# Recurrent heads in pairs: denominators from columns of ones, gate rows spread by DMA, and the value units moved between the convolved tiles

## The chip, the cores and the metric

One Trainium2 chip, one core of it. The metric is the device time of one execution in microseconds (us); lower is better. TensorE does the matmuls, VectorE, ScalarE and GpSimd the elementwise work, and DMA queues issued from SyncE and ScalarE move data between HBM and the on-chip memory SBUF. Matmul results land in one of eight PSUM banks.

## The reference, cut to what matters

A model of three blocks over 512 tokens of width 1024 runs in one kernel: a recurrent layer, a band attention layer, and a layer with differential and forgetting attention, each with a gated feed-forward part. The change lies in the first layer. There the input is normalised and projected to q, k, v, an output gate o, eight gate values per token and the queries of a small memory attention. q and k pass a causal convolution of four taps and a SiLU. Four heads of width 192 then run a stabilised mLSTM. In parallel form, with F the running sum of the log forget gates, a = i - F the gate column and M the running maximum of a:

```python
S[s, t] = (k_s . q_t) * 192**-0.5 * exp(-(M_t - a_s))     # for s <= t, else 0
num_t = sum_s S[s, t] * v_s
den_t = sum_s S[s, t]
h_t = num_t / max(|den_t|, exp(-(F_t + M_t)))             # then an RMS norm per head
out = h * rsqrt(mean(h*h) + 1e-6) * head_g * sigmoid(o)
```

The kernel normalises num itself with den inside the epsilon term, so that one root per head and token serves both. The memory attention is an ordinary softmax over 256 memory tokens for two pairs of heads. Its result and the four heads' outputs are concatenated and multiplied by w_out.

## The kernel before, in words

Tokens lie on the free axis (512) and features on the 128 partitions; only the value tiles have tokens on partitions. Large products run on f32 operands split into a high part (WH, hH) and a low part (WL, hL), three matmuls for each 128 rows. The weights come in units of 256 columns, loaded by SyncE into `raw`; ScalarE copies a unit into WH and VectorE writes WL, the difference (step `conv`, L1221 and L1578), two slots in turn. A feature-major tile (`fm`, L891) is 24 matmuls of 512 columns, a value tile (`tm`, L910) 48 matmuls of 256 columns.

A function `order()` writes one list of steps, and each engine walks through it and issues its own part of every step. So every engine's queue has the order of that list, and an engine that waits at a step holds all that it has behind it. Bank numbers are handed out in turn over eight banks, and TensorE waits until the engine that drained the bank's last content is through.

The steps around the change are these.
- `conv_in` for each tile of q and k: VectorE multiplies the PSUM tile by the norm factor (L1553), ScalarE starts the convolution (L1300), VectorE adds three taps (L1701). The SiLU (L1307) is put off to the end of the next tile.
- `probs`, `norm_p`, `turn`, `values`, `parts`: the memory attention. VectorE takes maxima (L1712) and negates them (L1731), ScalarE the exponentials (L1335), VectorE normalises (L1739, L1755), TensorE transposes (L1024), ScalarE and VectorE copy the two banks of it to SBUF (L1359, L1765), and TensorE multiplies by the values (L1044). `soft()` puts them between tiles of other work, as many tiles as its argument `per` says for each of four rounds.
- `gates_*`: four rows of gate values are worked out on four partitions; the E row is exp(-(F + M)).
- `m_scores` for a head: TensorE spreads the M row over 128 partitions by a matmul with one row of the identity (L1054) and computes the scores, pieces of 128 and 64 rows in turn (L1065); ScalarE copies the M row out, VectorE subtracts, ScalarE takes the exponential, VectorE multiplies it with the scores, GpSimd zeroes the upper triangle.
- `m_values`: TensorE multiplies by the values (L1086), by a matrix of ones for the denominators (L1093), and spreads the E row (L1100). `m_sums`: sums of squares over the head by a matmul with ones (L1110), then denominators, root and reciprocal (L1828). `gated`: the product with sigmoid(o), GpSimd (L2077), and its split.
- `out_first`: the first product with w_out (L835) over five of eight feature tiles, kept in four banks; `out_rest` adds the other three.

The work is done in this order: two tiles of q, two of k, two and two more, value units 0 and 1, q, k, then the heads one by one between value unit 2 and the six tiles of o.

Of the kernel before, what the change touches and what calls it, by code (L numbers as in the profile page):

```python
# [7 lines left out]
F32 = mybir.dt.float32  # L8
# [18 lines left out]
POS = {j: bi * 512 + off for j, L, bi, off in JL}  # L27
HALVES = ((0, 6, (4, 4, 4)), (6, 11, (4, 3, 3)))
# [14 lines left out]
def plan():  # L43
# [3 lines left out]
    u += [("a_w_in", 0, 0, 8, 256 * j, 256) for j in (0, 3, 1, 4, 6, 7, 2, 5, 8, 9, 10, 11)]  # L47
# [97 lines left out]
def order():  # L145
# [5 lines left out]
    def put(*x):  # L151
        steps.append(x)
# [209 lines left out]
    put("fence", "memA")  # L362

# [4 lines left out]
    gens = qk(0) + qk(1) + [g_tm(2, "mix0", "vA", "v")] + qk(2) + [g_tm(1, "mix0", "vA", "v", u0=2)]  # L368
# [8 lines left out]
    for hd in range(4):  # L377
        fill(gens, tiles[hd][0])
        if hd < 3:
            put("m_scores", hd + 1)  # L380
        fill(gens, tiles[hd][1])
        put("m_values", hd)
        deferred.append(("m_sums", hd))
        fill(gens, tiles[hd][2])
        if hd == 2:
            for t in range(3):
                put("gated", t)
# [151 lines left out]
def program(nc, wall, xt, memt, colsd, biasd, consts, rope, out):  # L539
    ctx = ExitStack()  # L540
    with ctx:
# [41 lines left out]
        vA = place("vA", [128, 4, 768])  # L583
# [3 lines left out]
        Mrow = place("Mrow", [4, 512])  # L587
        colA = place("colA", [128, 4, 4])
        Erow = place("Erow", [4, 512])
# [14 lines left out]
        top[0] = mark_M  # L604
        den = [place(f"den{i}", [128, 512]) for i in range(2)]
        fac = [place(f"fac{i}", [128, 512]) for i in range(2)]
        Mb = [place(f"Mb{i}", [128, 512]) for i in range(2)]
        Eb = place("Eb", [128, 1280])
        Pm = [place(f"Pm{i}", [128, 1280]) for i in range(2)]
# [55 lines left out]

        rows = nc.dram_tensor("rows", (8, 512), F32, kind="Internal").ap()
# [5 lines left out]
        gz, gt, ga, gm = O[0:4, 1, :], O[0:4, 2, :], O[0:4, 3, :], Mrow[:, :]  # L672
# [12 lines left out]
        s_rows = sem("rows")  # L685
        s_cols, s_K, s_RC, s_RS, s_out = (sem(n) for n in ("cols", "consts", "RC", "RS", "out"))
# [99 lines left out]
        def tensor(e):  # L786
# [52 lines left out]
            for what, *a in STEPS:  # L839
# [208 lines left out]
                elif what == "m_scores":  # L1048
                    hd = a[0]
                    b, before = bank(("mb", hd), ("Mb", hd))  # L1050
                    if before:
                        w.wait_ge(*at(*before))
                    w.wait_ge(*at("gateD", "mm"))
                    e.matmul(ps[b][:, :], ident[0:4, hd:hd + 1].broadcast_to([4, 128]), gm, start=True,  # L1054
                             stop=True).then_inc(*mark("mspread", hd))
                    ends = {bi: [x[0] for x in JL if x[2] == bi][-1] for bi in range(3)}
                    bs = [bank(("ms", hd, bi), ("mP", hd, ends[bi])) for bi in range(3)]
                    for j, L, bi, off in JL:
                        b, before = bs[bi]
                        if before:  # L1060
                            w.wait_ge(*at(*before))
                        for n, (t, r, _, _) in enumerate(pieces(hd)):
# [3 lines left out]
                                          q[r, t, j * 128:512], start=(n == 0), stop=(n == 1))  # L1066
                        mm.then_inc(*mark("mscores", hd, j))

                elif what == "m_values":
                    hd = a[0]  # L1070
                    P = Pm[hd % 2]
                    w.wait_ge(*at("mtri", hd, JL[-1][0]))
                    for t0 in (0, 2):
                        for un in range(192 * hd // 256, (192 * hd + 191) // 256 + 1):
                            w.wait_ge(*at("vev", "vA", t0, un))
                    for t, r, c0, width in pieces(hd):
                        if r.start == 64:
                            b = BANK[("mv", t)]
                            turns.append(b)
                        else:  # L1080
                            held = width == 64
                            b, before = bank(("mv", t), ("mnum", t, 64 if held else 0), hold=held)
                            if before:
                                w.wait_ge(*at(*before))
# [3 lines left out]
                        mm.then_inc(*mark("mvalues", t, r.start))  # L1088
# [1229 lines left out]
```

## Time and profile before

| | us |
|---|---|
| median of 3 runs | 1922.43 (1920.96 to 1923.5) |
| the profiled execution | 1919.19 |
| its span, first to last instruction | 1917.4 |
| TensorE busy | 1875.5 |
| VectorE busy | 927.4 |
| ScalarE busy | 753.3 |
| GpSimd busy | 277.8 |

The profile calls TensorE PE, its weight loads PEld, VectorE DVE, ScalarE ACT, GpSimd POOL and SyncE SP; L891 is line 891 of the kernel. A matmul in plain f32 leaves two records. A releaser behind an arrow is the instruction whose end let the idle engine go on.

### The profile page before, as it was taken

How to read it: one execution, taken by the hardware profiler on the slowest of the kernel's cores; microseconds unless marked ns; L12 is line 12 of the kernel's file. 1: busy time of each engine (PE TensorE's matmuls, PEld its weight loads, DVE VectorE, ACT ScalarE, POOL GpSimd, SP SyncE). 2: the span in 40 equal slices, each digit the busy share in tenths (PEclk: the TensorE clock that was granted, in tenths of full speed). 3: DMA queues.
4: the chain of work that ended last, by engine and by line, in shares of the span. 5: the costliest groups of instructions: out<-in, count | busy, mean ns of one | idle time of the engine just before them, and what ended most of it. 6: DMA issues, size and time to landing. Idle time of an engine off the chain costs nothing.

```text
span 1917.4 us, 21811 instructions
## 1 busy us (share of the span) xinstructions
PE 1875.5 (98%) x8962; PEld 1513.6 (79%) x8962; DVE 927.4 (48%) x1443; ACT 753.3 (39%) x1190; POOL 277.8 (14%) x239
## 2 busy tenths in 40 slices
PE   9989999999999999999999999999999999999998
PEld 7775568888888889667888888877887788888886
DVE  6754565544345343664545245355566443323324
ACT  5553444432133234574433133342457442312323
POOL 1001121221022110001222012122000122201210
PEclk9999999999999999999999999999999999999999
DMA  5121012222222333211232222222122123232221
GB/s 219 66 88 45 22 66 93 86 107 104 94 88 87 111 111 124 96 45 66 88 110 92 106 88 92 94 100 89 66 78 77 66 89 110 88 107 91 88 94 61
DMA packets 30754, 172.30 MB, mean 90 GB/s; under 512 B 3256, under 2 KB 5432, under 8 KB 12736
## 3 DMA queue, kind: packets, MB, share of 16 engines
q1 hardware_dynamic: 26320, 163.03, 23.9%
q10 hardware_dynamic: 4336, 7.88, 1.2%
q8 instruction: 71, 1.16, 0.2%
q14 instruction: 27, 0.22, 0.0%
HBM read 168.79 MB, written 2.11 MB: 89 GB/s over the span
## 4 chain that ended last, share of the span: by engine, by line
PE 88%; DVE 5%; ACT 4%; issue 1%; DMA 1%; POOL 0%; ACTq 0%; SPq 0%; DVEq 0%; POOLq 0%
PE ps L891 49%; PE ps L1148 18%; PE ps L835 6%; PE ps L910 5%; PE ps L1044 2%; PE ps L999 2%; DVE WL L1578 1%; PE ps L1065 1%; PE ps L1024 1%; PE ps L1086 1%; ACT PB L1335 1%; DMA raw<-in_wall 1%; ACT WH L1221 1%; PE ps L824 1%; PE ps L815 0%
## 5 line engine op out<-in xcount | busy, mean ns | idle before, releaser
L891 PE MATMUL ps<-hH,WH 128*128 128x512 f32 x1472 | 581.4, 395 | 7.0 <-DVE WL L1578 5.8
L891 PE MATMUL ps<-hH,WL 128*128 128x512 f32 x1472 | 573.7, 390 | 0.0
L891 PE MATMUL ps<-hL,WH 128*128 128x512 f32 x1472 | 573.5, 390 | 0.0
L1578 DVE TENSOR_TENSOR WL<-raw,WH 128x1024 fp32r<-128x1024 f32 (+2 forms) x312 | 382.2, 1264 | 375.7 <-ACT WH L1221 375.6
L1221 ACT ACTIVATE WH<-raw 128x1024 fp32r<-128x1024 f32 (+2 forms) x312 | 303.6, 1021 | 285.7 <-PE ps L1148 228.4
L891 PEld LDWEIGHTS ps<-hH,WH 128*128 128x128 f32 x1472 | 276.8, 188 | 76.4 <-issue 16.9
L891 PEld LDWEIGHTS ps<-hL,WH 128*128 128x128 f32 x1472 | 276.8, 188 | 58.8 <-issue 2.6
L891 PEld LDWEIGHTS ps<-hH,WL 128*128 128x128 f32 x1472 | 276.6, 188 | 58.1
L1148 PE MATMUL ps<-fH,WH 128*128 128x512 f32 x528 | 205.4, 389 | 0.0
L1148 PE MATMUL ps<-fL,WH 128*128 128x512 f32 x528 | 205.4, 389 | 0.0
L1148 PE MATMUL ps<-fH,WL 128*128 128x512 f32 x528 | 205.4, 389 | 0.0
L2093 POOL TENSOR_TENSOR Y<-Y,Rsb 128x512 f32<-128x512 f32 x66 | 85.2, 1292 | 548.3 <-ACT Y L1427 382.8
L1148 PEld LDWEIGHTS ps<-fH,WH 128*128 128x128 f32 x528 | 99.1, 188 | 20.6
L1148 PEld LDWEIGHTS ps<-fH,WL 128*128 128x128 f32 x528 | 99.1, 188 | 20.5
L1148 PEld LDWEIGHTS ps<-fL,WH 128*128 128x128 f32 x528 | 99.1, 188 | 20.5
L1437 ACT ACTIVATE fH<-Z 128x512 fp32r<-128x512 f32 x66 | 41.7, 632 | 186.1 <-DVE Z L1874 186.1
L2101 POOL TENSOR_TENSOR fL<-Z,fH 128x512 fp32r<-128x512 f32 x66 | 85.2, 1291 | 199.0 <-ACT fH L1437 199.0
L1553 DVE TENSOR_TENSOR GG<-ps,Rsb 128x512 f32<-128x512 f32 x66 | 45.5, 690 | 115.6 <-PE ps L891 107.3
L1874 DVE TENSOR_TENSOR Z<-ps,Y 128x512 f32<-128x512 f32 x66 | 45.3, 687 | 113.8 <-PE ps L891 108.2
L910 PE MATMUL ps<-WH,hH 128*128 128x256 f32 x320 | 92.8, 290 | 3.9 <-ACT PA L1335 3.9
L910 PE MATMUL ps<-WL,hH 128*128 128x256 f32 x320 | 91.2, 285 | 0.0
L910 PE MATMUL ps<-WH,hL 128*128 128x256 f32 x320 | 91.2, 285 | 0.0
(343 smaller groups left out, 2047.8 us busy)
## 6 DMA issues: line engine op xcount, KB each, us to landing
raw<-in_wall SPq DMA_DIRECT2D x140, 1024.0 KB, 4.6
raw<-in_wall SPq DMA_DIRECT2D x12, 768.0 KB, 3.9
bias<-in_bias ACTq DMA_DIRECT2D x12, 256.0 KB, 3.4
X<-in_xt SPq DMA_DIRECT2D x8, 256.0 KB, 9.6
CB<-rows ACTq DMA_DIRECT2D x8, 256.0 KB, 3.4
out_y<-X SPq DMA_DIRECT2D x3, 512.0 KB, 3.0
raw<-in_wall SPq DMA_DIRECT2D x4, 256.0 KB, 5.5
mrA<-in_memt ACTq DMA_DIRECT2D x4, 256.0 KB, 6.0
```

The source lines that it names most:

```text
L835: mm = e.matmul(ps[b][:, :], ww[:, k, c:c + 128], x, start=(k == seq[0] and i == 0), stop=(k == seq[-1] and i == 2))
L891: mm = e.matmul(ps[b][:, 0:N], ww[:, k, c:c + 128], x[:, k, 0:N], start=(k == 0 and i == 0), stop=(k == 7 and i == 2))
L910: mm = e.matmul(o, x[:, k, t * 128:t * 128 + 128], ww[:, k, :], start=(k == 0 and i == 0), stop=(k == 7 and i == 2))
L999: mm = e.matmul(ps[b][:, c:c + L], queries[u["kind"]][r, u["m"], t * 128:t * 128 + 128], keys[u["kind"]][r, u["m"], 0:L], start=opens, sto ...
L1148: mm = e.matmul(ps[b][:, :], ww[:, kx, mi * 128:mi * 128 + 128], x[:, k, :], start=(gi == 0 and kx == 0 and p == 0), stop=(gi == 2 and kx ...
L1221: e.activation(WH[n % NCV][:, c], raw[n % NRAW][:, c], ACT.Copy).then_inc(*mark("wh", n, x))
L1437: e.activation(F[i]["H"][:, k, :], F[i]["Z"][m % 2][:, :], ACT.Copy).then_inc(*mark("fH", i, int(half), k))
L1553: return e.tensor_tensor(dst, src, Rsb[rows, :], ALU.mult)
L1578: e.tensor_tensor(WL[n % NCV][:, c], raw[n % NRAW][:, c], WH[n % NCV][:, c].bitcast(F32), ALU.subtract).then_inc(*mark("wl", n, x))
L1874: e.tensor_tensor(F[i]["Z"][m % 2][:, :], ps[BANK[(name, m)]][:, :], F[i]["Y"][m % 4][:, :], ALU.mult).then_inc(*mark("fz", name, m))
L2093: e.tensor_tensor(y[:, :], y[:, :], Rsb[:, :], ALU.mult).then_inc(*mark("fy", i, m))
L2101: e.tensor_tensor(F[i]["L"][:, k, :], F[i]["Z"][m % 2][:, :], F[i]["H"][:, k, :].bitcast(F32), ALU.subtract).then_inc(*mark("fL", i, int(h ...
```

## The change

- The M and E rows are written to a small DRAM tensor and read back by DMA, spread over partitions, on ScalarE's queue (`m_rows`, `m_row`). The matmuls at L1054 and L1100 go.
- The value tile `vA` grows from 768 to 1024 columns. Beside each 64-wide piece of a head stand 64 columns of ones, so that the matmul of this piece gives the numerators on 64 partitions and the denominators on the other 64. The matmuls at L1093 go. The evacuation of the value tiles is cut where the ones stand (`V_PARTS`).
- Scores of two heads are computed together: first all 128-row pieces, then the 64-row pieces in turn between the two heads, which lie on different halves of the partitions.
- The sum of squares takes its second operand from `den`, half of which holds the squared denominator, scaled; the add on VectorE goes. `m_sums` is no longer put off, and `m_norm` is a step of its own.
- Three buffers for the products instead of two and a shared one; `m_prep` works out the exponentials ahead of the scores.
- The three value units stand between the q and k tiles; the rounds of the memory attention get other numbers of tiles, and the steps of the heads are written out. Two fences, at which engines waited for one another, go.

```diff
-    u += [("a_w_in", 0, 0, 8, 256 * j, 256) for j in (0, 3, 1, 4, 6, 7, 2, 5, 8, 9, 10, 11)]
+    u += [("a_w_in", 0, 0, 8, 256 * j, 256) for j in (0, 3, 6, 1, 4, 7, 2, 5, 8, 9, 10, 11)]
...
-        return [(t, slice(0, 128), 192 * hd, 128), (t + 1, slice(0, 64), 192 * hd + 128, 64)]
-    return [(t + 2, slice(0, 128), 192 * hd + 64, 128), (t + 1, slice(64, 128), 192 * hd, 64)]
+        return [(t, slice(0, 128), 256 * hd), (t + 1, slice(0, 64), 256 * hd + 128)]
+    return [(t + 2, slice(0, 128), 256 * hd + 128), (t + 1, slice(64, 128), 256 * hd)]
+V_PARTS = [(0, 0, 192, 0), (0, 192, 64, 320), (1, 0, 256, 384), (2, 0, 64, 640), (2, 64, 192, 832)]
+V_ONES = ((192, 128), (704, 128))
...
-            timed.extend([[1, ("gates_later",)], [2, ("gates_rest",)], [9, ("gate_columns",)]])
+            timed.extend([[1, ("gates_later",)], [2, ("gates_rest",)], [5, ("gate_columns",)], [6, ("m_rows",)]])
...
-    gens = qk(0) + qk(1) + [g_tm(2, "mix0", "vA", "v")] + qk(2) + [g_tm(1, "mix0", "vA", "v", u0=2)]
+    gens = qk(0) + vA(0) + qk(1) + vA(1) + qk(2) + vA(2) + [g_fm(3, "mix0", "o", "o")]
...
-    soft("A", gens, lambda p: (2, 2) if p < 3 else (2, 0), lambda p: conv_ahead(now["unit"] + 2) if p else None)
-    put("fence", "mlstm")
-    gens.append(g_fm(3, "mix0", "o", "o"))
-    tiles = ((0, 1, 0), (1, 1, 1), (0, 1, 1), (0, 0, 1))
+    def rows_out(p):
+        if p:
+            conv_ahead(now["unit"] + 2)
+        if p == 3:
+            for hd in (0, 1):
+                put("m_row", "M", hd)
+            put("m_row", "E", 0)
+    soft("A", gens, lambda p: ((1, 2), (2, 1), (1, 2), (1, 0))[p], rows_out)
+    put("m_prep", 0)
+    put("m_row", "E", 1)
+    put("m_row", "M", 2)
+    put("m_prep", 1)
+    put("m_row", "M", 3)
     put("m_scores", 0)
...
+    put("m_prep", 2)
+    fill(gens, 2)
+    put("m_values", 0)
+    put("m_values", 1)
+    put("m_prep", 3)
+    fill(gens, 2)
+    put("m_sums", 0)
+    put("m_sums", 1)
+    fill(gens, 1)
+    put("m_norm", 0)
+    put("m_norm", 1)
+    for hd in (2, 3):
+        put("m_row", "E", hd)
+    fill(gens, 1)
+    put("m_scores", 2)
+    fill(gens, 2)
+    put("m_values", 2)
+    put("m_values", 3)
+    fill(gens, 2)
+    put("m_sums", 2)
+    put("m_sums", 3)
+    for t in range(3):
+        put("gated", t)
+    fill(gens, 1)
+    put("m_norm", 2)
+    put("m_norm", 3)
     run_deferred()
     fill(gens, 99)
...
+                    for n in (0, 1):
+                        for hd, (j, L, bi, off) in ([(hd, v) for hd in (h0, h0 + 1) for v in JL] if n == 0 else
+                                                    [(hd, v) for v in JL for hd in (h0, h0 + 1)]):
...
+                            t, r, _ = pieces(hd)[n]
...
                             mm = e.matmul(ps[b][:, off:off + L], kk[r, t, j * 128:j * 128 + 128],
-                                          q[r, t, j * 128:512], start=(n == 0), stop=(n == 1))
+                                          q[r, t, j * 128:512], start=(n == 0 and off == 0),
+                                          stop=(n == 1 and j == M_ENDS[bi]))
...
-                            mm = e.matmul(ps[b][r, j * 128:512], vA[:, j, c0:c0 + width],
+                            mm = e.matmul(ps[b][:, j * 128:512], vA[:, j, c0:c0 + 128],
                                           P[:, POS[j]:POS[j] + 512 - j * 128], start=(j == 0), stop=(j == 3))
...
+                    w.wait_ge(*at("msqP", hd))
+                    e.matmul(ps[b][:, :], ones, msq[hd % 2][:, :], start=True, stop=False)
+                    w.wait_ge(*at("msqD", hd))
+                    w.wait_ge(*at("mden2", hd))
+                    e.matmul(ps[b][:, :], ones, den[hd % 2][:, :], start=False, stop=True).then_inc(*mark("msums", hd))
...
+                elif what == "m_rows":
+                    w.wait_ge(*at("gateD", "mm"))
+                    e.dma_start(m_rows[0:4, :], gm).then_inc(s_mrows, 16)
+                    w.wait_ge(*at("gateE"))
+                    e.dma_start(m_rows[4:8, :], gE).then_inc(s_mrows, 16)
...
+                            w.wait_ge(*at("mEbD", hd - 2, JL[-1][0]))
+                        e.dma_start(Mb[hd % 2][:, :], m_rows[hd:hd + 1, :].broadcast_to([128, 512])).then_inc(
+                            s_M[hd % 2], 16)
...
-                    e.activation(D, D, ACT.Square, scale=1e-3).then_inc(*mark("mden2", hd))
-                    w.wait_ge(*at("mfac", hd, 1))
-                    e.activation(Fc, Fc, ACT.Sqrt).then_inc(*mark("mfacA", hd))
+                    e.activation(den[hd % 2][r, :], den[hd % 2][r, :], ACT.Square, scale=3e-6 ** 0.5).then_inc(
+                        *mark("mden2", hd))
+                    w.wait_ge(*at("mfac", hd, 0))
+                    e.activation(fac[hd % 2][:, :], fac[hd % 2][:, :], ACT.Sqrt, scale=1.0 / 192).then_inc(
+                        *mark("mfacA", hd))
...
+                    e.tensor_scalar(fac[hd % 2][:, :], ps[BANK[("mq", hd)]][:, :], 192e-34, 192e35, ALU.max,
+                                    ALU.min).then_inc(*mark("mfac", hd, 0))
...
+                    for n, (c, size) in enumerate(V_ONES):
+                        e.memset(vA[:, :, c:c + size], 1.0).then_inc(*(mark("vones") if n else mark("vonesh")))
```

## Rows read from the trace of the kernel before

**Rows 1.** The page: busy us, share of the span, instructions; the last chain.
```profile
PE 1875.5 (98%) x8962; PEld 1513.6 (79%) x8962; DVE 927.4 (48%) x1443; ACT 753.3 (39%) x1190; POOL 277.8 (14%) x239
...
PE 88%; DVE 5%; ACT 4%; issue 1%; DMA 1%; POOL 0%; ACTq 0%; SPq 0%; DVEq 0%; POOLq 0%
```

**Rows 2.** TensorE's waits, 60 to 330 us: total us, times, longest.
```profile
PE ps L891 <- DVE WL L1578: 4.5, 2, 2.8
PE ps L910 <- ACT PA L1335: 3.9, 1, 3.9
PE ps L1044 <- DVE PTA L1765: 3.8, 1, 3.8
PE ps L1044 <- ACT PTA L1359: 1.7, 1, 1.7
PE ps L835 <- DVE WL L1578: 1.2, 1, 1.2
```

**Rows 3.** TensorE's timeline, 160 to 187 us: start, us, instruction.
```profile
160.35 1.12 PE L1054 MATMUL ps<-Mrow,K 4*128 4x512 f32 x2
161.40 5.95 PE L1065 MATMUL ps<-q,k 128*128 128x512 f32 x16
...
174.21 0.39 PE L910 MATMUL ps<-WH,hH 128*128 128x256 f32 x1
...
180.06 4.62 PE L1086 MATMUL ps<-Pm,vA 128*128 128x512 f32 x16
184.60 2.42 PE L1093 MATMUL ps<-Pm,K 128*128 128x512 f32 x8
186.96 1.12 PE L1100 MATMUL ps<-Erow,K 4*128 4x512 f32 x2
```

**Rows 4.** TensorE's timeline, one pair of band scores.
```profile
803.46 2.43 PE L999 MATMUL ps<-kB,qB 64*128 64x512 f32 x16
```

**Rows 5.** VectorE's timeline, 85 to 147 us.
```profile
85.95 0.68 DVE L1553 TENSOR_TENSOR sq<-ps,Rsb 128x512 f32<-128x512 f32 x1
...
93.57 0.17 DVE L1739 RECIPROCAL stA<-stA 128x4 f32<-128x4 f32 x1
...
96.09 2.35 DVE L1578 TENSOR_TENSOR WL<-raw,WH 128x1024 fp32r<-128x1024 f32 x2
98.36 1.28 DVE L1712 TENSOR_REDUCE stA<-ps 128x2 f32<-128x512 f32 x2
...
146.54 0.68 DVE L1765 COPY PTA<-ps 128x512 f32<-128x512 f32 x1
```

**Rows 6.** Stretches: busy us, then granted clock, DMA share, GB/s.
```profile
102.00:102.50 0.50, 0.50 (x4) 0.50 (x3) 0.00 (x0) 0.50 (x3) 0.00 (x0) 0.50 0.70 295
147.00:152.00 5.00, 4.63 (x20) 2.87 (x21) 3.18 (x4) 1.12 (x2) 0.00 (x0) 1.00 0.33 98
```

**Rows 7.** ScalarE's timeline, 99 to 116 us.
```profile
99.89 0.47 ACT L1335 ACTIVATE PA<-ps,stA 128x256 f32<-128x256 f32 x1 [5.39 <-DVE stA L1731]
...
103.40 0.24 ACT L1335 ACTIVATION_READ_ACCUMULATOR PA<-ps,stA 128x1 f32 x1
...
115.16 0.63 ACT L1294 ACTIVATE Erow<-O 4x512 f32<-4x512 f32 x1
115.70 0.80 ACT L1320 ACTIVATE vA<-ps,small 128x256 f32<-128x256 f32 x2
```

**Rows 8.** TensorE's timeline, values of memory pair 1 and tile k4.
```profile
147.37 1.94 PE L1044 MATMUL ps<-PTA,mvA 128*64 128x512 f32 x8 [3.80 <-DVE PTA L1765]
149.24 0.50 PE L891 MATMUL ps<-hH,WH 128*128 128x512 f32 x1
```

**Rows 9.** DMA issues: count, KB each, median us to landing.
```profile
CB<-rows ACTq DMA_DIRECT2D x8, 256.0 KB, 3.4
```

**Rows 10.** VectorE's timeline, normalising a head, and WL before the out tiles.
```profile
197.82 3.35 DVE L1828 RECIPROCAL fac<-fac 128x512 f32<-128x512 f32 x1 [0.69 <-ACT fac L1394]
...
277.44 3.78 DVE L1578 TENSOR_TENSOR WL<-raw,WH 128x1024 fp32r<-128x1024 f32 x2 [1.65 <-ACT WH L1221]
```

More of the change, by code:

```diff
@@ L685, in program @@
         s_rows = sem("rows")
+        s_mrows = sem("mrows")
+        s_M = [sem(f"M{i}") for i in range(2)]
+        s_E = [sem(f"E{i}") for i in range(2)]
         s_cols, s_K, s_RC, s_RS, s_out = (sem(n) for n in ("cols", "consts", "RC", "RS", "out"))
@@ L1048, in tensor @@
                 elif what == "m_scores":
[L1049 to L1062, printed above, removed]
+                    h0 = a[0]
+                    bs = {}
+                    for hd in (h0, h0 + 1):
+                        for bi in range(3):
+                            bs[hd, bi] = bank(("ms", hd, bi), ("mP", hd, M_ENDS[bi]))
+                    for n in (0, 1):
+                        for hd, (j, L, bi, off) in ([(hd, v) for hd in (h0, h0 + 1) for v in JL] if n == 0 else
+                                                    [(hd, v) for v in JL for hd in (h0, h0 + 1)]):
+                            b, before = bs[hd, bi]
+                            if before:
+                                w.wait_ge(*at(*before))
+                            t, r, _ = pieces(hd)[n]
                             w.wait_ge(*at("qk", "q", t))
@@ L1107, in tensor @@
                         w.wait_ge(*at(*before))
-                    for n, (t, r, _, width) in enumerate(pieces(hd)):
-                        w.wait_ge(*at("msqP" if width == 128 else "msqD", t, r.start))
-                        mm = e.matmul(ps[b][:, :], ones[r, :], sq[t % 2][r, :], start=(n == 0), stop=(n == 1))
-                        mm.then_inc(*mark("msums", hd, n))
+                    w.wait_ge(*at("msqP", hd))
[3 more added lines that the diff above has]
+                    e.matmul(ps[b][:, :], ones, den[hd % 2][:, :], start=False, stop=True).then_inc(*mark("msums", hd))
                 elif what in ("out_first", "out_rest", "out_all"):
@@ L1318, in scalar @@
                     p = ps[BANK[(name, t0, un)]]
+                    if name == "vA":
+                        for i in range(2):
+                            for n, (_, c, size, o) in enumerate([v for v in V_PARTS if v[0] == un]):
+                                last = i == 1 and c + size == 256
+                                e.activation(vA[:, t0 + i, o:o + size], p[:, 256 * i + c:256 * i + c + size],
+                                             ACT.Copy, scale=small[:, 4 + t0 + i:5 + t0 + i]).then_inc(
+                                    *(mark("vev", name, t0, un) if last else mark("vevh", name, t0, un, i, n)))
+                        continue
                     for i in range(2):
@@ L1827, in vector @@
                     w.wait_ge(*at("mfacA", hd))
-                    e.reciprocal(Fc, Fc).then_inc(*mark("mfac", hd, 2))
-                    w.wait_ge(*at("mfac", hd, 2))
-                    for t, r, _, width in pieces(hd):
-                        w.wait_ge(*at("msqP" if width == 128 else "msqD", t, r.start))
+                    e.reciprocal(Fc[:, :], Fc[:, :]).then_inc(*mark("mfac", hd, 1))
+                    w.wait_ge(*at("mfac", hd, 1))
+                    w.wait_ge(*at("msqP", hd))
@@ L1832, in vector @@
+                    for n, (t, r, _) in enumerate(pieces(hd)):
                         e.scalar_tensor_tensor(out=q[r, t, :], in0=q[r, t, :], scalar=col("hg", t, p=r),
                                                in1=Fc[r, :], op0=ALU.mult, op1=ALU.mult).then_inc(
[L1834 removed]
+                            *mark("mnorm", hd, n))
                 elif what == "gated":
@@ L2190, in program @@
                        for i, x in enumerate(CONV_SEQ)}
-        MSQ_SEQ = [(t, r.start, hd, n) for hd in range(4) for n, (t, r, _, _) in enumerate(pieces(hd))]
-        MSQ_BEFORE = {(t, r): [("cvD",) + CONV_SEQ[-1] + (3,), ("cvD",) + CONV_SEQ[-2] + (3,)] + [
-            ("msums", h2, n2) for t2, r2, h2, n2 in MSQ_SEQ if h2 < hd and t2 % 2 == t % 2]
-            for t, r, hd, n in MSQ_SEQ}
         ROPE_SEQ = [(n, m) for n in ("dq", "dk") for m in range(4)]
```

216 lines of the change are left out of this document (98 added, 118 removed).

## The prediction

> **What bounds the kernel now.** The page comes first: TensorE is busy 98% of the span and every other engine under half, and the chain that ended last is 88% TensorE [rows 1]. So a microsecond taken out of TensorE's stream counts, one taken from another engine counts only where TensorE waits for it. Next the list of TensorE's waits in the stretch that the change touches, 60 to 330 us [rows 2]: six waits, 15.1 us together. That is what reordering could win at most, besides matmuls that go.
>
> The profiled execution took 1919.2 us, its span being 1917.4; the median is 1922.4. The sum is made against the first and its difference is taken off the median.
>
> **What goes from TensorE's stream.** Matmuls overlap at their ends, so I price them from start to start. The stretch from 160 to 187 us shows each kind [rows 3].
> - The spread of the M row (L1054): 160.35 to 161.40, 1.05 us. Four heads, 4.20 us. A DMA takes its place.
> - The spread of the E row (L1100): the same operation and 1.12 us with its tail, as the other; 1.05 us, four times, 4.20 us.
> - The denominator matmuls with ones as weights (L1093): 184.60 to 186.96, 2.36 us, four times, 9.44 us. The values matmuls keep their number and columns. A piece 64 wide becomes one 128 wide, whose other half is ones; the 16 records of a head take 4.54 us now (180.06 to 184.60) though half of them are only 64 wide, so width costs nothing.
> - Scores: a head takes 5.88 us (5.95 less the 0.07 by which the next overlaps) for 2560 columns, of which the values matmuls make as many in 4.54. The old order alternates matmuls over 128 rows and over 64 rows. The new one runs both heads' 128-row pieces first: 2560 columns, which I price at 4.54. Then come the 64-row pieces, turn by turn on rows 0 to 63 and 64 to 127, each head in its own bank. The band scores in the second layer have exactly these lengths and this alternation: 2.43 us with the tail, 2.36 without, for 2560 columns, so two run side by side [rows 4]. A pair costs 6.90 instead of 11.76; two pairs save 9.72. Bounds: if the 64-row pieces don't overlap, 4.54 instead of 2.36, and the saving is 5.36; if nothing changes, 0.
> - Sums of squares: two matmuls of 512 columns before and after, one of them over 128 rows instead of 64; 0, by the values matmuls, which cost the same over half the width.
>
> Together 27.56 us.
>
> **The first waits stay.** Up to 69.16 us the queues are in the same order, so the 1.67 us wait for WL stays. Unit 6 is now value columns; unit 7's WL comes after both convolutions of k on VectorE as before and ends at 85.95 [rows 5]; TensorE can start at 85.05, with its first half, as before. It gets there after two value tiles (5.85 each, 174.21 to 180.06 [rows 3]), the scores of memory pair 1 (about 1.9) and the gate columns (0.4), at about 83.2. 1.8 instead of 2.82.
>
> **The value tile at 100.96** waited 3.87 us for exponentials, and after that idle time the granted clock was 0.50 up to 104.5, that is 1.2 instead of 2.4 GHz; matmuls came 0.21 us apart, against 0.12 later, some 16 of them, 1.5 us [rows 2, 6]. In the new order q2 stands there. The exponentials start right after VectorE's maxima and free the banks as TensorE needs them, about 0.4 us late.
>
> **The new stall: values of memory pair 0.** In step order the new kernel has q2, turn, q3, turn, values. The values wait for the last copy of turned probabilities on VectorE, which is queued behind two convolutions. The chain from VectorE's queue, all durations from [rows 5, 7]:
> - 85.95 WL of unit 7 done, where q2's product began before; 2.52 normalising pair 0 (93.57 to 96.09): 88.5; the maxima of pair 1, first half 1.28 and a negation 0.17: 90.0.
> - ScalarE: exponentials 3.6: 93.6; the value tile's evacuation, now four instructions, 1.2 (two take 0.80); E row's Exp 0.54; first half of WH of unit 8 1.0 (half of two halves at 2.0): 96.3. VectorE has idled since 91.4.
> - WL of unit 8 2.3 (96.09 to 98.36): 98.6; convolution q2 3.8 (85.95 to 93.57 are two): 102.4; copy 0.6; convolution q3 3.8; copy: values start 0.83 after that copy starts (146.54, 147.37), at 107.7 [rows 5, 8].
>
> TensorE is through with q3 and its turn at 98.5 (two tiles of 5.56, half of 149.24 to 160.35 [rows 3, 8], two turns of 0.8, the 0.4). Stall: 9.2 us, instead of 1.65. Before, two value tiles that cost VectorE nothing stood at this place. Bounds: 3.8 (only the last convolution is late, as at 147.37) and 12. I take 9.2, since each link has a row. Idle for so long, TensorE should come back at 1.2 GHz as at 100.96: 3.4 us at half rate, 1.7 us lost (0 to 3.4).
>
> The values of pair 1 waited 3.80 behind the convolution of q5 [rows 2]. Now the value tile precedes them; what is left is the copy, 0.8.
>
> **DMA rows.** Two stores and eight broadcasts issue on ScalarE's queue, whose eight CB issues have a median of 3.4 us to landing [rows 9]. M0 is issued near 130, VectorE needs it at 134; its exponential must anyway stand behind the value tile on ScalarE until 140, and the masked products are wanted only after q4 and q5, near 156. Hidden by those two tiles; without that cover 3.4 us a pair. The memsets of ones fit into GpSimd's free time before 14 us, ahead of its squares.
>
> **The sums.** They used to be put off by a tile. Now they follow k4, k5 at once, and the second matmul waits for ScalarE's square of the denominator. On ScalarE that stands behind the convolution of k5, whose first half waits for VectorE, busy with k4. From the rows: VectorE ends the masks of head 3 and WL 12 about 2.6 us before k5 is through, so k5's share begins 0.8 after it, ScalarE 0.7 later, then 0.8 and the square 0.6: the matmul 3 us after k5, of which 0.95 is the first matmul. Then head 1's square stands behind head 0's square root, which waits for a clamp on VectorE behind the rest of k5: another 1.7. Together 3.8. The second pair stands behind o3: product 0.7, sigmoid 0.6, square 0.6, then clamp 0.7, root 0.6, square 0.6: 1.1 and 1.2, 2.3. Bounds for both: 2 and 9.
>
> **Before the out tiles.** Normalising heads 2 and 3 takes 4.72 us each (reciprocal 3.35, two products of 0.69), and both are now queued on VectorE ahead of the product of o5; its sigmoid is ahead of WH of unit 17, and its WL took 3.78, beside GpSimd's gating of two tiles [rows 10]. From o4's end: product of o4 1.5 (behind WL 16), 9.4, product 0.7, sigmoid 0.6, WH's first half 1.1, WL 3.8: 17.1; TensorE has o5 and two out parts of 3.4 (15 matmuls, at 24 in 5.56): 12.4. Wait 4.7 instead of 1.24. Bounds 0 and 6.
>
> **Sum.** Waits before 15.1 + 1.5 for the clock = 16.6. After: 1.67 + 1.8 + 0.4 + 9.2 + 1.7 + 0.8 + 3.8 + 2.3 + 4.7 = 26.4. That is 9.8 more waiting against 27.6 less work: 17.7 us shorter. Profiled 1901.5, median 1904.7, rounded 1905.
>
> **Rivals.**
> 1. *Waits stay short.* If VectorE keeps up (3.8 and no clock loss at the values, 2.0 at the sums, 1.24 at the out tiles), new waits are 11.7: 4.8 less than before, 32.4 us saved, 1890. For it: the engines beside TensorE are under half busy. Against it: the queues are in order, and each link is in the rows. 0.12.
> 2. *The change doesn't do what it says: the 64-row pieces don't overlap.* 4.4 to 9.7 us less saved, 1909 to 1914. Against it: the band scores. 0.08.
> 3. *The clock costs more.* After each of the stalls at the values and the sums the clock is low, and for longer: if the values and a whole tile (7.4 us of work) run at half rate, 5.7 more are lost, and two further drops at the sums lose 1.7 each: 1914. For it: the drop after 3.87 us; against: none after 2.82 nor after 3.80 (1.00 from 147) [rows 6]. The Trainium skill (TensorE: Matmul & The Clock Gate, What's actually happening) calls the throttled state the default which activity releases, and that rule speaks against trading work for waiting; the trace agrees at 101 us and not at 147. By the rule taken at its strictest the sum would have these drops in it, by the row at 147 it has the first alone. 0.05.
> 4. *Slower: the DMA of a gate row holds VectorE.* M2 may be issued only after ScalarE's first two exponentials, near 140, and VectorE stands at its wait with WL 11, both convolutions of q and the denominators behind it. It should land near 144; VectorE turns to it at 147, unit 11 is wanted at 165 and its chain (masks 1.3, exponential 1.2, WH and WL 3.4) needs 6. So a landing by 159, 19 us after issue, costs nothing, each microsecond beyond is lost, and beyond 19 + 17.7 + 3.8 = 40.5 us from issue the kernel is slower; at 47 us it takes 1922.4 - 17.7 + 28 = 1933. Against it: 3.4 us in the median for the same broadcast of CB. 0.04.
>
> The forecast has 0.66 (1899 to 1909). 0.05 is left for several waits at the top of their bounds (2.8 at the values and 1.7 of clock, 2.9 in the sums, 1.3 at the out tiles give 1913) and for one that I don't see. A measurement of this kernel can tell 0.2%, 3.8 us. Within it fall 0.03 of that rest; slower are rival 4 and 0.01 of the rest: faster 0.92, same 0.03, slower 0.05. The range leaves out below most of rival 1 (0.10), above rival 4, most of the rest and part of rival 3 (0.10): 1895 to 1914.
>
> **What the profile after would show.** No spread or denominator matmuls; a scores pair near 6.9 us; TensorE idle about 9 us ahead of the first memory pair's values, then clock 0.5; short waits in the sums; first out matmul near 252 instead of 273.16. The prediction is wrong if the stall at the values is under 5 or over 12, or a pair of scores costs over 9.

## The result, and the profile after

The changed kernel takes 1901.28 us in the median of four runs (1900.84 to 1904.11); the kernel before, on the same chip, takes 1922.84, the median of its four. The ratio is 0.9893, interval [0.9875, 0.991]: 1.1% faster. A second measurement of the same kernel beside later experiments gave 0.9897 [0.9884, 0.9911]. The eight executions of the two measurements lie in two groups, four within 0.3 us of 1901.1 and four within 0.3 us of 1904.3. The forecast was 1905 with 1895 to 1914, and faster with a chance of 0.92. The matmuls that went and the places of the waits came as forecast; what the clock costs did not. The saving is 20.6 us by the ratio instead of 17.7.

The first lines of the page after, as [rows 1] of before: TensorE's busy time is down by 21.5 us, and its share of the last chain by two points, which went to VectorE.

```profile
PE 1854.0 (97%) x8914; PEld 1510.8 (79%) x8914; DVE 925.1 (49%) x1439; ACT 741.9 (39%) x1184; POOL 274.6 (14%) x241
PE 86%; DVE 7%; ACT 4%; issue 1%; DMA 1%; POOL 0%; SPq 0%; ACTq 0%; DVEq 0%; POOLq 0%
```

The list of TensorE's waits in the same stretch as [rows 2], with the same columns:

```profile
PE ps L1084 <- DVE PTA L1825: 8.8, 2, 8.0
PE ps L1136 <- ACT den L1449: 6.0, 4, 2.4
PE ps L875 <- DVE WL L1637: 5.0, 1, 5.0
PE ps L931 <- DVE WL L1637: 1.7, 1, 1.7
PE ps L950 <- DVE WL L1637: 1.7, 1, 1.7
```

The reader is to see that the waits grew from 15.1 to 23.2 us, and where: the values of the memory attention (L1084), the second matmul of the sums (L1136), the third out tile (L875). The gain has to be in the matmuls. The first matmul with w_out starts at 253.00 us in this profile and at 250.14 in the second one, where the forecast had 252 and the kernel before 273.16.

TensorE's timeline, to be read beside [rows 3] and [rows 8] (start, us, instruction):

```profile
98.54 1.04 PE L1064 MATMUL ps<-K,PA 128*128 128x128 f32 x8
107.53 3.68 PE L1084 MATMUL ps<-PTA,mvA 128*64 128x512 f32 x8 [7.95 <-DVE PTA L1825]
111.14 0.80 PE L931 MATMUL ps<-hH,WH 128*128 128x512 f32 x1
...
139.47 6.84 PE L1104 MATMUL ps<-q,k 128*128 128x512 f32 x32
146.24 0.50 PE L931 MATMUL ps<-hH,WH 128*128 128x512 f32 x1
...
157.27 8.79 PE L1123 MATMUL ps<-Pm,vA 128*128 128x512 f32 x32
...
165.82 0.48 PE L931 MATMUL ps<-hH,WH 128*128 128x512 f32 x1
```

A pair of scores takes 6.77 us (139.47 to 146.24), where two heads took 11.76. The values with their denominators take 8.55 for two heads (157.27 to 165.82), where one head's values, ones and E row took 7.95 (180.06 to 188.01, the latter 1.05 behind the last of [rows 3]). The values of memory pair 0 wait 7.95 us and then take 3.68 instead of the 1.94 of [rows 8].

VectorE's timeline ahead of that wait, beside [rows 5]: it is the chain of the prediction, link by link.

```profile
88.50 1.28 DVE L1772 TENSOR_REDUCE stA<-ps 128x2 f32<-128x512 f32 x2
...
96.22 2.36 DVE L1637 TENSOR_TENSOR WL<-raw,WH 128x1024 fp32r<-128x1024 f32 x2 [4.76 <-ACT WH L1246]
98.50 0.68 DVE L1612 TENSOR_TENSOR sq<-ps,Rsb 128x512 f32<-128x512 f32 x1
...
102.90 0.68 DVE L1612 TENSOR_TENSOR sq<-ps,Rsb 128x512 f32<-128x512 f32 x1
...
106.70 0.68 DVE L1825 COPY PTA<-ps 128x512 f32<-128x512 f32 x1
```

q2 was computed by TensorE long before 98.50, but its product stands behind WL of unit 8, which waited 4.76 us for ScalarE; ScalarE was at the exponentials of memory pair 1 until 93.8, then at the E row, the copies of the value tile and the first half of WH (95.14 to 96.2).

The new DMA rows, with the columns of [rows 9]:

```profile
Mb<-m_rows ACTq DMA_DIRECT2D x4, 256.0 KB, 4.8
den<-m_rows ACTq DMA_DIRECT2D x4, 128.0 KB, 3.1
```

And the granted clock in four stretches of this execution (columns as [rows 6]), then in six of the second profile of the same kernel, the same four and two that start earlier behind the same waits:

```profile
86.00:88.00 2.00, 2.00 (x7) 1.55 (x6) 1.93 (x10) 0.78 (x1) 0.00 (x0) 0.51 0.51 131
108.00:110.00 2.00, 2.00 (x6) 0.53 (x4) 1.97 (x9) 0.00 (x0) 0.00 (x0) 0.50 0.00 0
184.00:186.00 2.00, 2.00 (x5) 0.97 (x5) 0.20 (x1) 0.00 (x0) 0.00 (x0) 0.50 0.03 8
267.00:269.00 2.00, 2.00 (x6) 1.51 (x6) 0.00 (x0) 0.00 (x0) 0.00 (x0) 0.50 0.82 348
```

```profile
86.00:88.00 2.00, 2.00 (x11) 1.64 (x10) 1.95 (x8) 0.62 (x1) 0.00 (x0) 1.00 0.60 143
108.00:110.00 2.00, 2.00 (x8) 0.53 (x4) 1.97 (x8) 0.00 (x0) 0.00 (x0) 0.50 0.00 0
180.00:182.00 2.00, 2.00 (x3) 0.41 (x2) 1.49 (x3) 0.87 (x2) 0.00 (x0) 0.50 0.00 0
184.00:186.00 2.00, 2.00 (x19) 2.00 (x18) 0.69 (x1) 1.11 (x2) 0.00 (x0) 1.00 0.00 0
263.00:265.00 2.00, 2.00 (x6) 1.56 (x5) 0.72 (x2) 0.00 (x0) 0.00 (x0) 0.50 0.95 328
267.00:269.00 2.00, 2.00 (x10) 1.69 (x9) 0.00 (x0) 0.00 (x0) 0.00 (x0) 1.00 0.03 8
```

The clock is at 0.50 (1.2 GHz) after the waits of 8, 2.4 and 5.0 us in both executions, but it comes back sooner in the second. From 60 to 330 us it is low from 86 to 89.5, 103 to 113.5, 181.5 to 188.5 and 263.5 to 270.5 us in the first, and from 104.5 to 112, 179.5 to 183.5 and 261.5 to 265.5 in the second. Only the wait of 1.7 us ahead of q2 is followed by a low clock in one and by a full one in the other. The first profiled execution took 1904.11 us with a span of 1902.4; the second took 1901.00 with a span of 1899.3.

### The profile page after: what moved, and what is told of

The parts are those of the page before. It is cut to its first block, busy times and chain, and to the rows that moved or that the text cites. A ratio compares the mean times of both kernels' runs of the same rounds, so it can differ in the third digit from the quotient of the medians.

```text
span 1902.4 us, 21711 instructions
## 1 busy us (share of the span) xinstructions
PE 1854.0 (97%) x8914; PEld 1510.8 (79%) x8914; DVE 925.1 (49%) x1439; ACT 741.9 (39%) x1184; POOL 274.6 (14%) x241
## 4 chain that ended last, share of the span: by engine, by line
PE 86%; DVE 7%; ACT 4%; issue 1%; DMA 1%; POOL 0%; SPq 0%; ACTq 0%; DVEq 0%; POOLq 0%
PE ps L931 49%; PE ps L1173 18%; PE ps L875 6%; PE ps L950 6%; DVE WL L1637 2%; PE ps L1084 2%; PE ps L1039 1%; PE ps L1064 1%; PE ps L1123 1%; ACT PB L1400 1%; ACT WH L1246 1%; DMA raw<-in_wall 1%; PE ps L1104 1%; PE ps L864 1%; PE ps L855 0%
## 5 line engine op out<-in xcount | busy, mean ns | idle before, releaser
L1173 PEld LDWEIGHTS ps<-fH,WL 128*128 128x128 f32 x528 | 99.1, 188 | 20.6
L1612 DVE TENSOR_TENSOR GG<-ps,Rsb 128x512 f32<-128x512 f32 x66 | 45.5, 691 | 115.9 <-PE ps L931 107.5
```

The costliest lines, as they stand in the source:

```text
L1173: mm = e.matmul(ps[b][:, :], ww[:, kx, mi * 128:mi * 128 + 128], x[:, k, :], start=(gi == 0 and kx == 0 and p == 0), stop=(gi == 2 and kx ...
L1612: return e.tensor_tensor(dst, src, Rsb[rows, :], ALU.mult)
```

## The experiments

Each kernel ran four or five times (the first one eleven) beside the kernel before. Differences below are the difference of the ratios times 1922.5 us, and for the kernel after I take the mean of its two ratios, 0.9895. The intervals are about 0.0013 either way for each ratio, 2.5 us, so sizes of single steps come from the traces, and the times say whether anything hid them.

### Does the order gain anything by itself?

```diff
# on the kernel before
-    u += [("a_w_in", 0, 0, 8, 256 * j, 256) for j in (0, 3, 1, 4, 6, 7, 2, 5, 8, 9, 10, 11)]
+    u += [("a_w_in", 0, 0, 8, 256 * j, 256) for j in (0, 3, 6, 1, 4, 7, 2, 5, 8, 9, 10, 11)]
...
-            timed.extend([[1, ("gates_later",)], [2, ("gates_rest",)], [9, ("gate_columns",)]])
+            timed.extend([[1, ("gates_later",)], [2, ("gates_rest",)], [5, ("gate_columns",)]])
...
-    gens = qk(0) + qk(1) + [g_tm(2, "mix0", "vA", "v")] + qk(2) + [g_tm(1, "mix0", "vA", "v", u0=2)]
+    vA = lambda j: [g_tm(1, "mix0", "vA", "v", u0=j)]
+    gens = qk(0) + vA(0) + qk(1) + vA(1) + qk(2) + vA(2)
...
-    soft("A", gens, lambda p: (2, 2) if p < 3 else (2, 0), lambda p: conv_ahead(now["unit"] + 2) if p else None)
+    soft("A", gens, lambda p: ((1, 2), (2, 1), (1, 2), (5, 0))[p], lambda p: conv_ahead(now["unit"] + 2) if p else None)
```

> The kernel before with the new order alone: value units between the q and k tiles, gate columns after the sixth tile, rounds of the memory attention (1,2), (2,1), (1,2), (5,0) so that q4, q5, k4, k5 still stand ahead of the heads. All matmuls of before are kept. My theory (the gain is the matmuls that went, 27.6 us, less the waits that the order brings): the waits of the order are 1.7 + 1.7 + 8.0 + 0.9 ahead of the heads and up to 3.4 of clock, against 15.3 before with its clock, so the time is that of before within 2 us: 1921 to 1924. Rival (the order is what gains, since it puts light value tiles between convolutions): 5 to 14 us faster than before, 1909 to 1917.

Measured: 1921.16, ratio 0.9997 [0.9988, 1.0006]. TensorE's waits, 60 to 330 us:

```profile
PE ps L1045 <- DVE PTA L1766: 8.5, 2, 7.6
PE ps L892 <- DVE WL L1579: 1.7, 1, 1.7
PE ps L911 <- DVE WL L1579: 1.7, 1, 1.7
PE ps L836 <- DVE WL L1579: 1.2, 1, 1.2
```

The order trades the waits of [rows 2], 15.1 us, for 13.1 us with one of 7.6 among them, and gains nothing. The rival that the light value tiles between the convolutions pay is out. The long wait belongs to the order, since all matmuls of before are in this kernel.

This trace shows one thing more. Its execution took 1925.54 us, 4.4 above the median, and in it the clock fell where TensorE had no wait at all, in the scores of head 1 in the old sequence (the heads count from 0). Below are the scores, and the busy times and clock of two microseconds within them:

```profile
167.54 10.64 PE L1066 MATMUL ps<-q,k 128*128 128x512 f32 x16
```

```profile
172.00:174.00 2.00, 2.00 (x4) 0.50 (x2) 0.09 (x1) 1.98 (x3) 0.00 (x0) 0.50 0.00 0
```

It was low from 167.5 to 182 us, and the scores took 10.57 us (167.54 to 178.11) instead of 5.88. The one trace of the kernel before has no such drop.

### Scores nested as before

```diff
# on the kernel after
-                    for n in (0, 1):
-                        for hd, (j, L, bi, off) in ([(hd, v) for hd in (h0, h0 + 1) for v in JL] if n == 0 else
-                                                    [(hd, v) for v in JL for hd in (h0, h0 + 1)]):
+                    for hd, (j, L, bi, off) in [(hd, v) for hd in (h0, h0 + 1) for v in JL]:
+                        for n in (0, 1):
```

> The kernel after, but with the scores' matmuls nested as before (head, then piece of the triangle, then its 128-row and its 64-row part). My theory: a pair takes 11.76 us instead of 6.85, two pairs 9.8, nothing hides it: 1911. Rival (the two heads' time in the scores is filled by something else, or waits behind it shrink, as VectorE and GpSimd get more time): under 5 us slower, 1906 or less.

Measured: 1911.52, ratio 0.9941 [0.9927, 0.9954], 8.8 us slower than the kernel after. The pair is back at the price of before, and nothing hides it, so the rival is out:

```profile
139.71 11.72 PE L1103 MATMUL ps<-q,k 128*128 128x512 f32 x32
```

### 64-row pieces without taking turns

```diff
# on the kernel after
-                        for hd, (j, L, bi, off) in ([(hd, v) for hd in (h0, h0 + 1) for v in JL] if n == 0 else
-                                                    [(hd, v) for v in JL for hd in (h0, h0 + 1)]):
+                        for hd, (j, L, bi, off) in [(hd, v) for hd in (h0, h0 + 1) for v in JL]:
```

> The kernel after, with all 128-row pieces first, but then the 64-row pieces of one head after those of the other instead of in turn. My theory (only matmuls on different halves of the rows, in different banks, run side by side): the second phase takes 4.5 us instead of 2.3, 2.2 more a pair, 4.4 together: 1905.7. Rival (what gained was only the missing change between 128 and 64 rows): within 1 us of the kernel after.

Measured: 1903.51, ratio 0.9901 [0.9888, 0.9915], 1.2 us slower than the kernel after, which the intervals can't tell from nothing. The trace can:

```profile
138.60 8.45 PE L1103 MATMUL ps<-q,k 128*128 128x512 f32 x32
...
143.01 4.04 PE L1103 MATMUL ps<-q,k 64*128 64x512 f32 x16
146.97 0.50 PE L931 MATMUL ps<-hH,WH 128*128 128x512 f32 x1
```

8.37 us for the pair against 6.77: taking turns is worth 1.6 a pair, 3.2 together, where I expected 4.4. The second line is the part of the first group from 143.01 us on, all 64-row pieces, which take 3.96 us; in the kernel after they take 2.36, 143.88 to 146.24:

```profile
143.88 2.43 PE L1104 MATMUL ps<-q,k 64*128 64x512 f32 x16
```

The 128-row pieces ahead of them take 4.41 in both. The two ideas in the scores so split as 3.4 a pair for keeping 128-row and 64-row matmuls apart (11.76 to 8.37) and 1.6 for running two halves side by side. The rival was right that the first is the larger part.

### Denominator matmuls and spreads put back

```diff
# on the kernel after, at the end of TensorE's m_values
+                    b, before = bank(("mx", hd), None)
+                    if before:
+                        w.wait_ge(*at(*before))
+                    for j in range(4):
+                        e.matmul(ps[b][:, j * 128:512], ones, P[:, POS[j]:POS[j] + 512 - j * 128],
+                                 start=(j == 0), stop=(j == 3))
# the second experiment has these instead of the four matmuls
+                    for i in (0, 1):
+                        e.matmul(ps[b][:, :], ident[0:4, hd:hd + 1].broadcast_to([4, 128]),
+                                 K[0:4, 0:4, :].rearrange("p i c -> p (i c)"), start=True, stop=True)
```

> The kernel after, with the four denominator matmuls with ones put back for each head into a bank that nobody reads (redundant work). My theory: 2.36 us a head, nothing hides it, 9.4 together, less at most 0.5 where the waits at the sums shrink: 1910.5. Rival (part of it falls into waits that follow, since VectorE catches up meanwhile): 4 to 7 us slower.

Measured: 1909.8, ratio 0.9931 [0.9918, 0.9943], 6.9 us slower than the kernel after. In its trace the ones of head 0:

```profile
161.81 2.32 PE L1130 MATMUL ps<-Pm,K 128*128 128x512 f32 x8
...
163.97 4.48 PE L1123 MATMUL ps<-Pm,vA 128*128 128x512 f32 x16
```

2.16 us (161.81 to 163.97) instead of the 2.36 of [rows 3]; four times 8.6. The waits at the sums are 5.6 instead of 6.0, and the other waits of the stretch are unchanged. The time alone doesn't decide: 6.9 with 2.5 either way holds my 8.9 and the rival's 4 to 7. The trace speaks for mine, since no wait gave back more than 0.4.

> The kernel after with two redundant spreads of a row by a matmul over four rows put back for each head, into a bank that nobody reads. My theory: 1.05 us each, eight of them 8.4 us, less up to 1 where the waits at the sums shrink: 1909. Rival (they fall into idle time of TensorE): under 4 us slower.

Measured: 1908.9, ratio 0.9936 [0.9922, 0.995], 7.9 us slower. A pair of spreads:

```profile
160.79 1.98 PE L1130 MATMUL ps<-K 4*128 4x512 f32 x4
162.70 4.58 PE L1123 MATMUL ps<-Pm,vA 128*128 128x512 f32 x16
```

1.91 us for two, 0.96 each instead of 1.05; eight are 7.6. The rival's 4 us are out. Both theories' sizes were a tenth too high, but neither kind of matmul falls into idle time.

### The values of memory pair 0 behind a tile

```diff
# on the kernel after, in soft()
+            late = stage == "A" and p == 2
-            if p >= 2 and not early:
+            if p >= 2 and not early and not late:
                 put("values", stage, p - 2)
                 put(us[p - 2]["sink"][0], stage, us[p - 2]["sink"][1], p - 2)
             first, second = per(p)
             fill(gens, first)
+            if late:
+                put("values", stage, p - 2)
+                put(us[p - 2]["sink"][0], stage, us[p - 2]["sink"][1], p - 2)
```

> The kernel after, with the values of memory pair 0 put behind the tile k2 instead of ahead of it. My theory (the 8 us of idle TensorE are the rest of VectorE's queue of two convolutions, and a tile of 5.6 us fits into them): wait 2.4 us instead of 8.0, and the clock stays up there, 1.7 to 2.8 more; k2's own convolution comes no later: 6 to 8 us faster than the kernel after, 1894. Rival (VectorE is the bound of this stretch, so the wait goes to the next turn or tile): under 2 us faster.

Measured: 1895.35, ratio 0.986 [0.9846, 0.9875], 6.7 us faster than the kernel after. Its wait list has for both values

```profile
PE ps L1088 <- DVE PTA L1829: 3.4, 2, 2.5
```

so 8.0 became 2.5, which is the 5.6 of a tile, and no other wait took its place. The copy on VectorE is at the same time as before; only TensorE has something to do until then.

The second half of my theory failed in this trace. The clock was low again, from 107 to 111 us, and the values took 3.5 us (107.52 to 111.05) as in the kernel after:

```profile
107.52 3.60 PE L1088 MATMUL ps<-PTA,mvA 128*64 128x512 f32 x8 [2.54 <-DVE PTA L1829]
```

So what this move gave in this execution is the wait and the full rate of k2, which now stands ahead of it (0.3 to 1.0 us, by the next experiment), and not the values' 1.7.

### Idle time filled with matmuls that nobody reads

```diff
# on the kernel after, ahead of the same values
+        if p == 2:
+            put("warm", 8)
...
+                elif what == "warm":
+                    b, before = bank("warm", None)
+                    if before:
+                        w.wait_ge(*at(*before))
+                    for i in range(a[0]):
+                        e.matmul(ps[b][:, :], ones, K[:, 0:4, :].rearrange("p i c -> p (i c)"), start=True, stop=True)
```

> The kernel after, with eight matmuls of 512 columns on constants into an unread bank (redundant work, about 7.3 us) in the idle time ahead of the values of memory pair 0. My theory: they end before the wait does, so the wait ends at the same time, and the granted clock is 1.00 in the values and in k2, where it is 0.50 for some 5 us: 1.7 to 2.7 us faster, 1899. Rival A (idle time there costs nothing but itself): no difference. Rival B (they delay the values): up to 2 us slower.

Measured: 1899.93, ratio 0.9884 [0.9869, 0.9899], 2.1 us faster than the kernel after by its mean ratio; the intervals overlap. The trace shows the clock part alone:

```profile
99.66 7.03 PE L917 MATMUL ps<-K 128*128 128x512 f32 x16
107.76 1.94 PE L1093 MATMUL ps<-PTA,mvA 128*64 128x512 f32 x8 [1.07 <-DVE PTA L1834]
```

```profile
108.00:110.00 2.00, 2.00 (x10) 0.67 (x7) 1.97 (x9) 0.26 (x1) 0.00 (x0) 1.00 0.00 0
```

The values start at 107.76, where they started at 107.53, and the copy on VectorE ahead of them is later by the same 0.2; they take 1.94 instead of 3.68 at full clock. k2 takes 5.58 us, where the two profiles of the kernel after have 6.61 and 5.83. So the idle time costs 1.7 us at the values and 0.3 to 1.0 in k2 on top of itself.

### Squares ahead of the tile

```diff
# on the kernel after; the Square on ScalarE becomes a step of its own
     put("m_prep", 3)
-    fill(gens, 2)
+    fill(gens, 1)
+    put("m_square", 0)
+    put("m_square", 1)
+    fill(gens, 1)
     put("m_sums", 0)
...
     put("m_values", 3)
-    fill(gens, 2)
+    fill(gens, 1)
+    put("m_square", 2)
+    put("m_square", 3)
+    fill(gens, 1)
```

> The kernel after, with ScalarE's squares of the denominators as a step of their own between the two tiles ahead of the sums (k4 and k5, o2 and o3). My theory (the second matmul of the sums waits for ScalarE's queue order, not for its work): the four waits of 6.0 us together go, and the low clock after the first pair with them, 1 to 2: 6 to 8 us faster, 1894. Rival (the waits are VectorE's lateness and move to the score products): under 2 us faster.

Measured: 1893.82, ratio 0.985 [0.9834, 0.9867], 8.7 us faster than the kernel after. The waits at the sums are gone from the list:

```profile
PE ps L1090 <- DVE PTA L1834: 8.9, 2, 8.0
PE ps L881 <- DVE WL L1646: 5.0, 1, 5.0
...
```

The two waits of 1.7 us stay, and the clock has no drop at the first sums (in the kernel after it fell there in both profiles). These are the same operations, by the same engine, at another place in its queue.

### Head 3 normalised behind the first out tile

```diff
# on the kernel after
     put("m_norm", 2)
-    put("m_norm", 3)
     run_deferred()
     fill(gens, 99)
     early = [out_first("A")]
     fill(early, 1)
+    put("m_norm", 3)
```

> The kernel after, with the normalising of head 3 put behind the first out tile, so that the product of o5 and WL of unit 17 stand ahead of it on VectorE. My theory: the wait of 5.0 us before the third out tile goes, and the low clock after it (5.8 us at half rate, 2.9), but the last two gated tiles come some 3 us later and may cost 0 to 2 at the first out_rest: 5 to 8 us faster, 1895. Rival (the wait moves whole to out_rest, which needs head 3): within 1 us.

Measured: 1894.57, ratio 0.9856 [0.9841, 0.9871], 7.5 us faster than the kernel after. VectorE, after the product of o5:

```profile
250.87 0.68 DVE L1612 TENSOR_TENSOR O<-ps,Rsb 128x512 f32<-128x512 f32 x1
253.19 2.36 DVE L1637 TENSOR_TENSOR WL<-raw,WH 128x1024 fp32r<-128x1024 f32 x2 [1.65 <-ACT WH L1246]
255.47 3.35 DVE L1886 RECIPROCAL fac<-fac 128x512 f32<-128x512 f32 x1
```

WL of unit 17 no longer stands behind the second reciprocal. It takes 2.36 us instead of 3.72; in the kernel after GpSimd's gating of two tiles ran beside it (260.23 to 263.70), here GpSimd is idle meanwhile. The wait of 5.0 us is gone and none stands at the out tiles, so head 3 is in time for them.

### All three together

> The kernel after with the three moves together: values of memory pair 0 behind k2, squares ahead of the second tile before the sums, the normalising of head 3 behind the first out tile. Alone they gained 5.9, 7.5 and 6.7 us. My theory (three separate waits at three places, each with its own low clock): the gains add up, less 2 us where two of them share a stretch at low clock: 1881 to 1884. Rival (with one wait gone, a later one grows, since ScalarE and VectorE have the same work to do in less time): 1886 to 1892.

Measured: 1879.35 (1879.0 to 1880.53), ratio 0.9773 [0.9759, 0.9786], 23.5 us faster than the kernel after and 2.3% faster than before. Alone the three gained 22.9 by the same reckoning. What is left of TensorE's waits in the stretch:

```profile
PE ps L1094 <- DVE PTA L1838: 3.8, 2, 2.4
PE ps L941 <- DVE WL L1650: 1.7, 1, 1.7
PE ps L960 <- DVE WL L1650: 1.7, 1, 1.7
```

The gains add up; the rival of waits that come back later is out. The values took 1.94 us this time, at full clock, after a wait of 2.4 us, where with that move alone they had a low clock after 2.5; in this stretch of the trace the clock is low only from 86 to 90 us. The mean granted clock of this profile is 0.996, against 0.989 and 0.993 in the two of the kernel after.

### The kernel after again

> The kernel after, unchanged, as the measure for its neighbours. The granted clock falls after short waits in some executions and not in others, so single executions may lie 3 us apart; the median should be 1901 within 1.

Measured: 1904.22 (1901.0 to 1904.53), ratio 0.9897. The median was 3 us above the first one's and missed the expectation: here three executions of four lie near 1904, in the first measurement three of four near 1901. Its profile is of one near 1901 (1901.00, mean granted clock 0.993); the executions near 1904 have 0.989. In this profile TensorE started the third out tile after the same 5.0 us of waiting, also at half clock, which was full again after 3.2 us (262.06 to 265.2) instead of 5.4.

## Why the prediction was right

**The matmuls that went.** I had 27.6 us. By the traces: M spreads 4.2; values, ones and E rows 4 x (7.95 - 4.28) = 14.7, where I had 13.6; scores 2 x (11.76 - 6.77) = 10.0, where I had 9.7: 28.9. The term sized too low is the values: "the values matmuls keep their number and columns" put them at 4.54 a head, and they take 4.28. I had concluded that width costs nothing from the time of a group that mixes both widths. The experiments show the counterpart: ones and spreads, put in among matmuls of the new kernel, cost 2.16 and 0.96, not 2.36 and 1.05. The missing 0.2 and 0.1 look like the price of a change of shape, which the mixed sequence of before paid; that reading is argued from these prices and the scores, and isn't shown: no run changed the width alone.

**Interleaved scores.** The band scores were the right row: 6.90 forecast, 6.77 measured, with the 64-row pieces at 2.36 as forecast and the 128-row pieces at 4.41 instead of 4.54. Nesting as before costs 8.8 us of time. The bound "if the 64-row pieces don't overlap, 4.54" was too high; without turns they take 3.96. Of its two parts, taking turns was to be worth 2.2 a pair and is worth 1.6; no longer alternating between 128 and 64 rows was to be worth 2.7 and is worth 3.4.

**The long wait.** Forecast from 98.5 to 107.7, 9.2 us; measured 99.6 to 107.5 in the one profile and 99.4 to 107.4 in the other, 8.0 us. The end came from a chain of nine durations in VectorE's and ScalarE's queues, and was 0.2 to 0.3 off. The start was 1.1 and 0.9 off: q2 ran at low clock in the one profile (7.14 us instead of 5.56), and in the other TensorE waited 1.2 us for exponentials behind it, where I had 0.4. That both come to nearly the same start of q3 (93.0 and 92.8) is chance: the first shows no wait for the exponentials. That order alone makes this wait and that a tile in front of the values takes 5.6 off it are both shown by runs.

**The clock.** This is the term that was mis-sized. I priced one drop at 1.7. The one after 8 us is in both profiles of the kernel after, in the order alone (after 7.6 us) and gone in the filled version; but the waits at the sums and the out tiles, for which I had put nothing, are followed by a low clock in both profiles too. By the same matmuls at full clock the losses are, as estimates, in the first profile 1.6 us in q2, 1.7 in the values, 1.0 in k2, 2.8 in the sums and the value tiles behind them and 2.6 in the third out tile, about 9.8 together. In the second they are nothing in q2, then 1.7, 0.3, 1.7 and 1.5, 5.2 together. So the mechanism of the rival "the clock costs more" was at work, with 3.5 and 8.1 us beyond my 1.7 where it had 9.1. Over all traces that have them, the clock was low after every wait of 7.6 us and more (nine of nine) and of 4.9 to 5.0 us (nine of nine), at the first sums after the wait of 2.4 us in five of seven, and behind the 1.7 us ahead of q2 in eight of twelve. And in the order alone it fell with no wait.

**The sums and the out tiles.** 6.1 forecast, 6.0 and 5.3 measured in the two profiles; 4.7 forecast, 5.0 measured in both. Both were read as queue order, not as work, and moving the steps removed them whole.

**DMA rows.** Forecast hidden. The M rows take 4.8 us to land instead of the 3.4 of CB, VectorE waits 1.4 us for one of them, and TensorE for none. By the prediction's own reckoning there were 19 us of room.

**The sum.** In the spans, 1917.4 less 1899.3 is 18.1 for the second profile, and 15.0 for the first with its low clock; the forecast for the profile was 17.7. That it lies between the two is in part luck: 1.3 us more went from the matmuls than forecast and the waits are 0.9 to 1.5 us shorter than the 24.7 that I had without the clock, against the 3.5 and 8.1 that the clock cost beyond its 1.7. And between 330 and 1890 us, where nothing was changed, the clock was low for 6.8 us in each profile of the kernel after and for 10.3 us in the one of before. By the ratio of the executions the saving is 20.6. The profiled execution of before, 1919.2, was below all the timed ones of its kernel, so the difference of two profiles understates the gain by 2 to 3 us. Which part of before was quicker in that execution isn't known, since it is the only trace of that kernel. Its mean granted clock was 0.995, in its other executions 0.991 to 0.995; a drop inside the scores like that of the order alone could account for it, but no trace of before shows one.

The rival "waits stay short" failed for the kernel after as the rows said, yet the three moves reach the 1890 it promised and more, 1879: these waits were not work that VectorE could not do in time.

## What to carry to other kernels

When one engine is busy 98% of the time, price each change as matmuls from start to start, and then walk the in-order queues of the other engines through the new order, step by step: the waits fell within 1.3 us of that walk. Then price the clock behind each wait that the walk finds, not only behind the longest: here 5.2 to 9.8 us, where one drop of 1.7 was counted. A step that only one late engine needs should stand in the list behind the next piece of TensorE's work; three such moves were worth 23.5 us, more than the 20.6 of the change itself. Take the price of a matmul from a row with its own shape and its own neighbours, not from a mixed group.

## What the runs showed of the hardware that I had not expected

- Alternating f32 matmuls over 128 and 64 rows cost 11.76 us a pair, grouped ones 8.37, grouped and in turn on two halves of the rows 6.77, for the same 5120 columns.
- Matmuls over 64 rows took 3.96 us for 2560 columns where those of one head follow those of the other, and 4.41 over 128 rows in the same sequence.
- After the same waits the low clock lasted twice as long in one execution as in another of the same kernel: 181.5 to 188.5 us against 179.5 to 183.5 after 2.4 us, 263.5 to 270.5 against 261.5 to 265.5 after 5.0 us. After 1.7 us it was 0.50 in one and 1.00 in the other.
- The clock also fell with TensorE never idle: 0.50 from 167.5 to 182 us in the order alone, while matmuls over 128 and 64 rows alternated, which took 10.57 us instead of 5.88.
